# A transformer stack in float32: norm statistics, root spreading, modulation schedule and scan buffers

## The reference, cut to what matters

```python
def _rms_norm(x, g):
    y = x * lax.rsqrt(jnp.mean(x * x, axis=-1, keepdims=True) + EPS)
    return y * g
# first block, layers 0 and 1 (attention mixers, relu-squared MLP of width 4096)
mx = (jax.nn.silu(c) @ ada_w[i] + ada_b[i])[:, None, :]       # six vectors of 1024
sx1, cx1, gx1, sx2, cx2, gx2 = jnp.split(mx, 6, axis=-1)
hx = hx + gx1 * mixer(_rms_norm(hx, norm1_g[i]) * (1 + cx1) + sx1)
hx = hx + gx2 * _mlp(_rms_norm(hx, norm2_g[i]) * (1 + cx2) + sx2, mlp_w1[i], mlp_w2[i])
# second block, layers 2 and 3: mixer = convolution, dilated attention and a gated scan; MLP of width 2816
# with a 3-tap convolution and gelu(gate) * val; between the blocks and at the end a plain norm
def step(state, inp):                       # the scan, chunk by chunk, both directions
    qt, kt, vt, bt = inp                    # bt: cumulated log gates of the chunk
    diff = bt[:, :, :, None, :] - bt[:, :, None, :, :]
    decay = jnp.where(lower, jnp.exp(jnp.where(lower, diff, 0.0)), 0.0)
    scores = jnp.einsum('bhtk,bhsk,bhtsk->bhts', qt, kt, decay)
```

## Time and profile before

| | us |
|---|---|
| median of three runs | 3849.35 (3847.57 to 3849.86) |
| the profiled execution | 3850.07, its span 3848.3 |
| TensorE busy | 3576.7 (93%) |
| VectorE busy | 2075.3 (54%) |
| GpSimd busy | 1186.9 (31%) |
| ScalarE busy | 916.0 (24%) |
| mean granted TensorE clock | 0.961 of full |

### The profile page before, as it was taken

How to read it: one execution, slowest core, us unless ns; L and a number is a source line. 1 busy time by engine, 2 the same in 40 slices (tenths; PEclk the granted TensorE clock), 3 DMA queues, 4 the chain that set the end, 5 groups by cost and what they waited for, 6 DMA issues and landing times. The chain is left out here.

```text
span 3848.3 us, 43150 instructions
## 1 busy us (share of the span) xinstructions
PE 3576.7 (93%) x15798; PEld 2637.7 (69%) x15798; DVE 2075.3 (54%) x3664; ACT 916.0 (24%) x1975; POOL 1186.9 (31%) x1162
## 2 busy tenths in 40 slices
PE   6999999999989999999989967899998995799998
PEld 4688655555546965788855557588884565658887
DVE  6575455544452274455644378278763457725654
ACT  2067221000020063211120343122212153222211
POOL 1000122232231032344430036256541005525554
PEclk9999999999999999999989977999999997899999
DMA  6300223233321100244432100134442200022222
GB/s 226 116 11 1 67 76 116 103 110 115 104 95 55 45 1 23 99 154 153 155 117 74 59 1 1 45 126 148 153 147 87 77 34 1 1 71 87 86 87 77
DMA packets 88783, 317.57 MB, mean 83 GB/s; under 512 B 10560, under 2 KB 10848, under 8 KB 88576
## 3 DMA queue, kind: packets, MB, share of 16 engines
q1 hardware_dynamic: 61920, 218.34, 17.4%
q10 hardware_dynamic: 24768, 90.19, 6.4%
q0 software_dynamic: 1888, 6.29, 0.6%
HBM read 312.68 MB, written 2.10 MB: 82 GB/s over the span
## 5 line engine op out<-in xcount | busy, mean ns | idle before, releaser
L1069 PE MATMUL ps<-arena 128*128 128x256 f32 (+1 forms) x3552 | 900.7, 407 | 17.8 <-issue 14.4
L599 PE MATMUL ps<-hbuf,ring 128*128 128x512 f32 (+1 forms) x2080 | 813.3, 554 | 28.7 <-ACT hbuf L1435 26.0
L1069 PEld LDWEIGHTS ps<-arena 128*128 128x128 f32 x3552 | 674.7, 190 | 209.3 <-issue 22.9
L599 PEld LDWEIGHTS ps<-hbuf,ring 128*128 128x128 f32 x2080 | 398.6, 192 | 438.2 <-issue 421.0
L2293 POOL TENSOR_TENSOR arena<-ring,arena 128x512 f32<-128x512 f32 (+1 forms) x132 | 169.6, 1285 | 767.5 <-PE ps L1069 767.5
L1758 DVE CUSTOM_DVE_ANT_0 aring<-aring,csil,adab 128x1024 f32<-128x1024 f32 x176 | 275.2, 1581 | 1.7
L1069 PE MATMUL ps<-arena,ring 128*128 128x256 f32 (+1 forms) x1040 | 273.9, 406 | 2.0 <-ACT arena L1364 2.0
L2253 POOL TENSOR_TENSOR arena<-arena 128x512 f32<-128x512 f32 (+1 forms) x48 | 71.7, 1493 | 572.7 <-ACT arena L1320 571.7
L1069 PEld LDWEIGHTS ps<-arena,ring 128*128 128x128 f32 x1040 | 197.4, 190 | 57.9 <-ACT arena L1364 4.1
L903 PEld LDWEIGHTS ps<-arena 128*128 128x128 f32 x1440 | 176.3, 193 | 85.0 <-ACT arena L1259 61.3
L903 PE MATMUL ps<-arena 128*128 128x128 f32 x1440 | 206.0, 287 | 19.9 <-ACT arena L1273 12.4
(11 more groups left out here) (267 smaller groups left out, 4949.3 us busy)
## 6 DMA issues: line engine op xcount, KB each, us to landing
aring<-in_ada ACTq DMA_DIRECT2D x172, 512.0 KB, 4.5
ring<-in_mlp SPq DMA_DIRECT2D x128, 512.0 KB, 3.8
ring<-in_up SPq DMA_DIRECT2D x88, 512.0 KB, 3.3
ring<-in_in SPq DMA_DIRECT2D x56, 512.0 KB, 3.2
ring<-in_out SPq DMA_DIRECT2D x32, 512.0 KB, 3.2
ring<-in_down SPq DMA_DIRECT2D x32, 512.0 KB, 3.5
ring<-in_odd_in SPq DMA_DIRECT2D x24, 512.0 KB, 3.2
arena<-in_ada SPq DMA_DIRECT2D x16, 512.0 KB, 13.8
```

What stands on the lines that cost most here:

```text
L599: mm = nc.tensor.matmul(slot[:, lo:hi], ring[:, c % RING, k, :], src[:, kt, lo:hi], start=kt == 0, stop=kt == nkt - 1)
L1069: mm = nc.tensor.matmul(ps[:, bank, 0:tw], w, x, start=start and j == 0, stop=j == len(pairs) - 1, skip_group_check=True)
```

## The change

1. In every norm but the first GpSimd adds blocks 1 to 5; the squares of blocks 6 and 7 go straight to TensorE, in both sums of the double norm.
2. The roots are spread by transposes of a broadcast column where a matmul with the identity stood; also in the first norm.
3. In the MLPs the rows of modulation are shared out over the first N-3 passes, and so are their fetches. ScalarE squares the blocks of pass n-1 in step n, no longer those of pass n-2; the last pass as before at the end.
4. In the scan the halves of WL are swapped between directions. VectorE makes the level exponents of the first unit before it cumulates units 1 to 5, and ScalarE exponentiates them before it copies pairs.
5. At the norm in front of layer 1 GpSimd waits for all updates of X before it starts four small loads.

```diff
@@ TensorE, norm
-                    pe.wait_ge(sq_summed, (KT - 2) * n)
+                    pe.wait_ge(sq_summed, (KT - 3) * n)
...
-                    pe.wait_ge(sqg_summed, KT - 2)
+                    pe.wait_ge(sqg_summed, KT - 3)
...
-                    pe.wait_ge(sqg_ready, KT)
+                    for j in range(KT - 2, KT):
+                        pe.wait_ge(sqg_ready, j + 1)
+                        for t in range(nt):
+                            nc.tensor.matmul(slot[:, 8 + t:9 + t], SQG[:, j % 2, t * P:(t + 1) * P], ones[:, 0:1], start=False,
+                                             stop=j == KT - 1, skip_group_check=True)
+                for j in range(KT - 1 if i == first0 else KT - 2, KT):
+                    pe.wait_ge(sq_ready, KT * n + j + 1)
+                    last = H[:, j, :] if i == first0 else SQ[:, j % 2, :]
                     for t in range(nt):
...
-                    mm = nc.tensor.matmul(slot[:, t * P:(t + 1) * P], roots[:, 1, t:t + 1].broadcast_to([P, P]), ident[:, :],
-                                          start=True, stop=True)
+                    mm = nc.tensor.transpose(slot[:, t * P:(t + 1) * P], roots[:, 1, t:t + 1].broadcast_to([P, P]), ident[:, :])
@@ TensorE, scan
-                                mm = nc.tensor.matmul(ps[:, 2 + v % 2, t * P:(t + 1) * P], WL[:, 7 * d + li, t * P:(t + 1) * P],
+                                mm = nc.tensor.matmul(ps[:, 2 + v % 2, t * P:(t + 1) * P], WL[:, 7 * (1 - d) + li, t * P:(t + 1) * P],
@@ ScalarE, quick
-                        fetch_mods(mod_share(i, n - 2, N))
+                        fetch_mods(mod_share(i, min(n - 2, N - 4), N - 3) if n < N - 1 else ())
...
-                    if n >= 2 and L[n - 2].last:
-                        squares(n - 2)
+                    if n and n < N and L[n - 1].last:
+                        squares(n - 1)
                     if n < N:
                         keep_u3(n)
-                fetch_mods(mod_share(i, N - 1, N))
                 squares(N - 1)
@@ ScalarE, scan
                 end_decays(0)
+                level_decays(0)
                 for u in range(6):
...
-                    if u == 0:
-                        level_decays(0)
                     end_decays(u + 1)
@@ VectorE, quick
-                    if n < N and (n or i != cond2_phase):
-                        modulate(mod_share(i, n, N))
+                    if n < N - 3 and (n or i != cond2_phase):
+                        modulate(mod_share(i, n, N - 3))
@@ VectorE, scan
                 cumulate(0)
                 end_exponents(0)
-                cumulate(1)
+                level_exponents(0)
                 weigh_ends(0)
-                for u in range(2, 6):
+                for u in range(1, 6):
                     cumulate(u)
-                level_exponents(0)
                 weigh_levels(0)
@@ GpSimd
-                        if 0 < j < KT - 1:
+                        if 0 < j < KT - 2:
                             add_square(next_norm(i), j, cols)
...
                 if i == first1:
+                    pool.wait_ge(resid_ready, KT * norm_phases.index(i))
                     load(COS, a["cos"], layer_in)
```

28 lines of the change are left out of this document (11 added, 17 removed).

## The result

The changed kernel takes 3805.55 us (median; 3800.3 to 3807.01) beside 3848.46 us (3845.59 to 3849.86) of the kernel before: ratio 0.9885, 95% interval 0.9873 to 0.9897, so 42.9 us (1.1%) less. The forecast was 3797.2 in a range of 3786 to 3811: the sign and the range hold; the gain was put at 52.2 and is 9.3 smaller. The profiled execution took 3804.49 (span 3802.7), 45.6 less than that of before.

A forecast was written before the change was run, and what follows sets the result against it. TensorE, busy 93% of the span, bounds the kernel; its holes are at four MLP ends and two scans. 39.6 + 7.3 - 2.1 - 0.9 + 1.3 + 7.0 = 52.2 us off 3849.35 gives 3797.2, range 3786 to 3811.

The forecast's parts named there:

- The ends of the MLPs: Four stretches from the last pass but one to the root: stacked waits go, saving 8.0, 16.9, 9.6 and 5.1 us.
- (a): Last MLP passes: squares one step earlier end the stall of GpSimd's adds and TensorE; stalls and half-clock aftermath 19.9 us.
- (b): Last MLP passes: VectorE's modulations, the first reduction 2.17 us, delay the next square; moved to earlier passes at cost 0.
- (c): MLP ends: GpSimd's adds end last, 5.30 us TensorE idle; block 6's 1.28 us add becomes column matmuls that fit.
- Spreading the roots: Norms behind the MLPs: one transpose a tile replaces two instructions, saving 2.1, 2.2, 1.5 and 1.5 us, 7.3 taken.
- The clock behind the norms: Behind the second MLP's norm: full clock is luck of the moment, expected lost once the norm is shorter, costing 2.1 us.
- Rival 2: Scan cumulations slowed beyond what they cover, transposes leave half clock behind three further norms: 13.3 us less gain, 3810.5; chance 0.12.
- The scans: Exponents first, cumulations cover the exponentials: 3.9 us a scan less slowing beside GpSimd; 3.5 a scan taken, 7.0 in all.
- the lower case: Scans: cumulations slowed beside GpSimd's queries by 0.3 us each, 4.8 over 16, leaving a gain of 2.3 a scan.
- rival 1: MLP ends: earlier squares wait for VectorE and hold the copy keep_u3, so the stall stays; 3817 us, chance 0.06.
- Rival 3: MLP passes: modulations packed in fewer passes make VectorE late for TensorE, up to 2.17 us a pass; 3934, chance 0.02.
- Rival 4: Four MLP ends: loads for the next phase end last, so the ends give nothing; 39.6 us less, 3836.8, chance 0.02.

The follow-up runs named there:

- E5: The changed kernel with its roots spread by products again instead of transposes; 8.2 us slower than the changed kernel by the medians.
- E7: The kernel before with only ScalarE's squares one step earlier; 32.4 us less than the kernel before.
- E6: The kernel before with only the modulations taken out of the last three MLP passes; 11.7 us less by the medians.
- E8: The kernel before with earlier squares and no modulation in the last three MLP passes, last but one square still added by GpSimd; 33.9 us less.
- E4: The kernel before with only the last two squares sent straight to TensorE; nothing gained, ratio interval 0.9997 to 1.0015.
- E3: The kernel before with earlier squares, no late modulation, last two squares straight to TensorE and GpSimd's wait ahead of four loads; 32.3 us less.
- E10: The changed kernel, GpSimd again adding the last but one square behind projections and for the doubled norm's plain sum, scaled sums first; 9.0 us less than the changed kernel.
- E1: The kernel before with only the exchanged level buffers and the new order in the scans; 6.7 us less.
- E2: The kernel before with only the roots spread by transposes; 6.0 us less.
- E9: The changed kernel with GpSimd's first level queries of a scan waiting until VectorE has ended the cumulations; 3801.29 us.
- E11: E10 plus identity products on TensorE, into a bank nobody reads, in the norms' holes; 3.7 us less than E10 by the medians.

## Why the prediction was right, and where it was off

**The ends of the MLPs: 39.6 forecast, 35.6 seen.** The three waits were named rightly and the sum nearly fits: with the clock at its best the same kernel's stretches are 46.2, 34.8, 24.6 and 24.6 (E5), against 46.4, 33.8, 24.3 and 24.3. What the forecast didn't see is that the waits are one chain. ScalarE's late square (a) pushes GpSimd's adds, those push the weight sums, TensorE, VectorE's update and the next square. By the stretches (a) alone is 29.0 (E7) and not the 19.9 that stood ahead of the last products; (b) alone is 12.2 and on top of (a) 8.2 (E6, E8); (c) alone is 4.7 and on top of both 0.8, less 2.4 behind the projections (E4, E3). Each of these singles carries up to 1.4 us of clock. The sum came near because the whole chain was costed at once; its parts, taken singly, were not worth what (a), (b) and (c) say. The step that failed is in (c): "its add (...) becomes one more set of column matmuls (...), which fit between the last product and the last square". In the doubled norm they don't fit: TensorE is busy without a break from the last product to the root, for 7.2 us (the forecast's own tail of 5.45 for this norm already counted three of the six sets behind the last square but one).

**What the four ends came short by**, 1.1, 2.3, 0.3 and 0.3. The doubled norm's tail was put at 5.45 with sets of 0.9. TensorE makes six sets between 1952.22 and 1959.57, the last two at 1.8 each, 1.7 more in all, because the clock falls in the middle of them. The same in the first MLP's norm, where 24 products of one column took 4.14 us and 2.82 at full clock (E10). In the other three some 0.3 to 0.5 us stands ahead of the last product, which waits for VectorE's update: that takes 1.47 beside GpSimd's add (1.02 in the fourth MLP) instead of the 0.48 that the forecast took from the earlier trace rows. That row is an update that reads its product from PSUM, the accumulator memory, and it ran at 0.48 while GpSimd was adding. The form that reads both from SBUF, the on-chip memory that the program calls arena, stood 1.3 us ahead of it in the same timeline of the kernel before:
```profile
3833.12 1.28 DVE L1842 SCALAR_TENSOR_TENSOR resid<-arena,mod,resid 128x256 f32<-128x256 f32 x1
```
The adds now stand beside it because the squares come earlier: what a faster ScalarE triggers, the forecast checked on ScalarE and TensorE and not on VectorE. A slip inside the working: two products of 2.58, 0.5 and 0.25 are 5.9 and not the 6.25 of the first MLP; 6.2 was seen.

**Spreading the roots: 7.3 + 1.3 + 3 x 0.6 = 10.4 forecast, 8.9 in the profile, 6 to 8 in the medians.** Four transposes at full clock are 0.65 (0.60 forecast). At the norms behind the first and the second MLP the spread's clock was half before and is half after, so that they save 1.39 and 1.46 and not the 2.1 and 2.2 that hung on the clock being full; that case stood in the forecast as "at half clock throughout 0.9 to 1.7" and should have been the value taken.

**The clock behind the norms: 2.1 forecast at the doubled one, 2.0 seen from its first product to the next attention, and 1.4 more behind the first MLP's.** The size is right and the reason isn't: the forecast called the full clock luck of the moment, which a shorter norm would end. It is full in seven of the eight kernels with products, E3, E5 and E7 with their shorter ends among them, and in none of the four with transposes alone (E5 above). So the 2.1 came in at its place through the transposes, which the forecast had set apart as a thing of which "No row here separates it" was said. The rule of the Trainium skill (TensorE: Matmul & The Clock Gate, Part 4: PE-mode transpose), by which a transpose doesn't count for the clock as a matmul does, agrees with the traces at the doubled norm and gains no support behind the first MLP's; that it is the cause is not shown, since the transposes also take less time. Rival 2's whole 13.3 us is refuted by E1 and E2, though the part of it that E2's trace shows, 2.5 us behind the doubled norm, was real: more than the 2.1 that the forecast had there.

**Norms behind the projections**: 0.8 for the set (0.9 forecast) less 0.6 for the spread, right.

**The scans: 7.0 forecast, 7.4 in the profile, 6.7 alone.** Right in size, though 3.5 was only the middle of two cases, 2.3 and 4.7, of which neither was argued to be the likelier. Both had a part of the truth: the cumulations are slowed (20 x 0.18 = 3.6 us, E9), but the level exponents behind them then run beside a GpSimd that has already made its first queries and waits, twelve of the fourteen at 0.41 each instead of 0.67. With the cumulations slowed as the lower case had it, 3.7 was gained and not 2.3.

**Rivals 1 and 3.** No copy (keep_u3) waited for a square: rival 1 is refuted. Rival 3 is refuted in size and not in kind. In the third MLP two passes take 12.24 and 12.16 us where all such passes took 12.09 before, 0.2 us in all; all eight kernels with the packed modulations show it and none of the five others does, so the "I cost the move at 0" was 0.2 short (what TensorE waited for in them is not shown), and one of the forecast's own signs of being wrong, a pass in the middle of an MLP that is longer than before, did show. Rival 4 is refuted by the four stretches.

**The rest** of the profile's shortfall of 6.6 us: 4.0 at the ends, 1.5 in the spreads, 1.3 of clock behind the norms, less 0.6 in which scans and projection norms were better than forecast, is 6.2. What is left, 0.4, is smaller than what the clock does in stretches that nobody changed. The attentions of layers 3 and 2, busy time by stretch, before:
```profile
3117.41:3178.53 61.12, 54.63 (x320) 37.56 (x319) 46.04 (x88) 40.44 (x94) 0.00 (x0) 1.00 0.00 1
2186.82:2249.63 62.81, 56.31 (x320) 38.15 (x319) 46.04 (x88) 40.44 (x94) 0.00 (x0) 0.97 0.00 1
```
and after:
```profile
3077.84:3141.82 63.98, 57.49 (x320) 38.87 (x319) 46.03 (x88) 40.48 (x94) 0.00 (x0) 0.95 0.00 1
2163.84:2224.98 61.14, 54.65 (x320) 37.58 (x319) 46.03 (x88) 40.50 (x94) 0.00 (x0) 1.00 0.00 1
```
The same 320 matmuls, 88 and 94 operations beside them: one attention lost 2.86 us and the other won 1.67, and of what the rows show only the granted clock differs. In the thirteen profiled kernels layer 3's stretch is 61.1, 62.8 or 64.0 us long (the table's last column), without regard to what was edited. The further 2.7 us between the profiled gain (45.6) and that of the medians (42.9) are within what executions of one kernel differ by (3800.3 to 3807.01).

## What to carry to other kernels

Waits that stand one behind the other in a loop of several engines are one chain: price the whole chain at its first link, and give the others only what is left once the first is gone. Here one moved statement on ScalarE gave three quarters of what the three edits gave together in the four stretches. Handing a reduction from GpSimd to TensorE pays only where TensorE stands still long enough for the added products, counted at the lower clock; on top of the other two edits it gave 0.8 us at two of the four ends, nothing at the other two, and took 0.8 in each of three other norms. And an edit worth a few us is read from the length of the stretch that it changes, together with the granted clock in it and beside a stretch that nobody touched, never from the difference of two spans.

## What was not expected of the hardware

- The granted clock fell in the middle of a string of one-column products without a hole: behind the last product of the second MLP sixteen of them took 2.23 us (clock 0.85) and the next sixteen 3.55 us (0.50). It doesn't always fall in one: in E10, 36 such products behind the first MLP ran at 1.00. In E11, with products of 128 columns added in the holes, the clock stayed at 1.00 behind the doubled norm.
- The clock behind the doubled norm goes with how the roots are spread: 1.00 in seven of eight kernels that spread by products, 0.63 to 0.72 in the four that spread by transposes.
- A cumulation (TENSOR_TENSOR_SCAN, 128x128) takes 0.35 us alone and 0.53 beside GpSimd's products, and moving them apart moved the loss of 3.5 us a scan to other VectorE operations, to within 0.02 us.
- VectorE's update that reads its product from SBUF rose from 0.48 us to 1.47 beside GpSimd adds of 1.26 and 1.45. The one that reads it from PSUM stayed at 0.48 beside an add (at 3834.44 in the kernel before).
